# Low parts of five weights moved to POOL and new keys turned into rows on VectorE, in a two-layer streaming encoder step on one Trainium2 core

## The reference

```python
def _layer(x, l, P, past_k, past_v, s_gla0, s_ret0):
    h = _rms_norm(x, P['ffn1_norm_pre'][l])
    x = x + 0.5 * _rms_norm(_swiglu(h, P['ffn1_w_up'][l], P['ffn1_w_down'][l]), P['ffn1_norm_post'][l])
    h = _rms_norm(x, P['mix_norm_pre'][l])
    m, k_rows, v_rows, s_gla, s_ret = _mixer(h, l, P, past_k, past_v, s_gla0, s_ret0)
    x = x + _rms_norm(m, P['mix_norm_post'][l])
    h = _rms_norm(x, P['ffn2_norm_pre'][l])
    x = x + 0.5 * _rms_norm(_swiglu(h, P['ffn2_w_up'][l], P['ffn2_w_down'][l]), P['ffn2_norm_post'][l])
    return x, k_rows, v_rows, s_gla, s_ret
```

## Time and profile before

| | us |
|---|---|
| median of 3 runs | 1318.64 |
| lowest, highest | 1318.46, 1318.78 |
| the profiled execution | 1318.82 |
| its span, first to last instruction | 1316.8 |
| TensorE busy in it | 1304.0 |
| VectorE busy | 829.1 |
| ScalarE busy | 632.5 |
| POOL busy | 131.5 |

### The profile page before, as it was taken

How to read it: one execution, slowest core, us unless ns; L and a number is a source line. 1 busy time by engine, 2 the same in 40 slices (tenths; PEclk the granted TensorE clock), 3 DMA queues, 4 the chain that set the end, 5 groups by cost and what they waited for, 6 DMA issues and landing times.

```text
span 1316.8 us, 24524 instructions
## 1 busy us (share of the span) xinstructions
PE 1304.0 (99%) x9456; PEld 1277.6 (97%) x9456; DVE 829.1 (63%) x1303; ACT 632.5 (48%) x1013; POOL 131.5 (10%) x176
## 2 busy tenths in 40 slices
PE   9999999999999999999999999999999999999998
PEld 8999999998999999999999999999989999999998
DVE  7755644687776955553486556337867778565672
ACT  6544443654556644443464444337535575444432
POOL 1000000450011200000030000005400130000000
PEclk9999999999999999999999999999999999999999
DMA  8555565463344555455545555545533355555552
GB/s 230 162 170 166 152 179 145 133 164 81 97 120 128 151 149 154 144 148 148 152 128 145 154 147 154 155 141 148 133 95 95 92 140 174 153 147 147 143 147 82
DMA packets 352026, 187.39 MB, mean 142 GB/s; under 512 B 9016, under 2 KB 348788, under 8 KB 351960
## 3 DMA queue, kind: packets, MB, share of 16 engines
q1 hardware_dynamic: 348376, 177.78, 47.9%
q0 software_dynamic: 2800, 7.85, 1.8%
q10 hardware_dynamic: 784, 0.86, 0.2%
HBM read 180.82 MB, written 4.33 MB: 141 GB/s over the span
## 4 chain that ended last, share of the span: by engine, by line
PE 93%; DVE 4%; POOL 1%; DVEq 1%; ACT 1%; issue 0%; POOLq 0%
PE ps L717 27%; PE ps L718 27%; PE ps L719 27%; PE ps L741 1%; PE ps L744 1%; PE ps L737 1%; POOL x L581 1%; PE ps L1027 1%; DVE w_l L573 1%; PE ps L1072 1%; PE ps L1096 1%; PE ps L952 1%; PE ps L1003 0%; PE ps L922 0%; PE ps L791 0%
## 5 line engine op out<-in xcount | busy, mean ns | idle before, releaser
L717 PE MATMUL ps<-xn_l,w_h 128*128 128x320 f32 x1696 | 531.9, 314 | 0.0
L719 PE MATMUL ps<-xn_h,w_h 128*128 128x320 f32 x1696 | 523.1, 308 | 0.0
L718 PE MATMUL ps<-xn_h,w_l 128*128 128x320 f32 x1696 | 523.0, 308 | 0.0
L573 DVE TENSOR_TENSOR w_l<-raw,w_h 128x1024 fp32r<-128x1024 f32 (+1 forms) x336 | 400.9, 1197 | 139.0 <-ACT w_h L561 138.6
L561 ACT ACTIVATE w_h<-raw 128x1024 fp32r<-128x1024 f32 (+1 forms) x336 | 346.1, 1034 | 208.8 <-DMA raw<-in_ffn_w_down_dram 127.7
L717 PEld LDWEIGHTS ps<-xn_l,w_h 128*128 128x128 f32 x1696 | 318.7, 188 | 3.7 <-issue 1.0
L718 PEld LDWEIGHTS ps<-xn_h,w_l 128*128 128x128 f32 x1696 | 318.7, 188 | 0.8
L719 PEld LDWEIGHTS ps<-xn_h,w_h 128*128 128x128 f32 x1696 | 318.5, 188 | 0.0
L719 PE MATMUL ps<-hid_h,w_h 128*128 128x320 f32 x704 | 217.0, 308 | 0.0
L717 PE MATMUL ps<-hid_l,w_h 128*128 128x320 f32 x704 | 217.0, 308 | 0.0
L718 PE MATMUL ps<-hid_h,w_l 128*128 128x320 f32 x704 | 217.0, 308 | 0.0
(11 more groups left out here) (310 smaller groups left out, 1265.5 us busy)
## 6 DMA issues: line engine op xcount, KB each, us to landing
raw<-in_ffn_w_up_dram SPq DMA_DIRECT2D x172, 512.0 KB, 3.8
raw<-in_ffn_w_down_dram SPq DMA_DIRECT2D x64, 448.0 KB, 3.7
raw<-in_w_in_dram SPq DMA_DIRECT2D x52, 512.0 KB, 3.8
...
```

The costliest lines, as they stand in the source:

```text
L573: dve.tensor_tensor(w_l[s][:, 0:cols], raw[s][:, 0:cols], w_h[s][:, 0:cols], ALU.subtract).then_inc(w_lo, 1)
L717: pe.matmul(out, w_h[s][:, w], xl, start=first, stop=False)
L718: pe.matmul(out, w_l[s][:, w], xh, start=False, stop=False)
L719: return pe.matmul(out, w_h[s][:, w], xh, start=False, stop=last)
```

## The change

- VectorE makes the token rows of the new keys. The new entry `rows` n transposes, in blocks of 32x32, 32 features of two heads' keys for all tokens: four instructions for the prompt (one for each 32 tokens of a block) and two for the sample. Eight entries, `rows` 0 to 7, take the place of `tok` 0 to 3. POOL's stores wait for `rows` 7 as well as for `tok` 7.
- POOL makes the low parts of tiles 18, 20, 22, 24 and 26, each in its queue at the end of tile n - 5. VectorE waits for POOL's counter before it makes the next tile's low part, and counts `w_lo` up for both, so that it stays in order. VectorE's low part of output tile 1 (number 28) moves behind `att_a` 9.
- `ret_dec` stands ahead of k-blocks 0 to 5 of tile 13 and of level 8. Tile 14 is cut at 4 and 6, not at 2 and 5.
- In `opening` and in `out`, TensorE waits for the low parts tile by tile and not for all four; in the mixer's opening `stat_x` stands two k-blocks later.
- In a spread the third matmul, which is for the sample's block, has 64 columns and not 128.
- At the start of the kernel the first gains are transposed and copied ahead of the first block of x, and two small loads are issued behind the first piece of the sample's x.

The diff, cut to its core:

```diff
+POOL_LOW = (18, 20, 22, 24, 26)
 ...
-       ("part", 12, 3, 8), ("level", 7), ("ketok",), ("part", 13, 0, 5), ("level", 8), ("ret_dec",), ("part", 13, 5, 8),
+       ("part", 12, 3, 8), ("level", 7), ("ketok",), ("ret_dec",), ("part", 13, 0, 5), ("level", 8), ("part", 13, 5, 8),
...
-    + [("att_t", 8), ("att_s", 10), ("att_a", 9), ("tok", 7)] + P8[25][:1] + [("att_o", 8), ("squares", "b")] + P8[25][1:]
+    + [("att_t", 8), ("att_s", 10), ("att_a", 9), ("tok", 7)] + P8[25][:1] + [("att_o", 8), ("squares", "b"), ("rows", 6)] + P8[25][1:]
...
                 for kind, *arg in SCHEDULE:
                     n = arg[0] if arg else None
-                    if kind == "weight":
+                    if kind == "part" and arg[2] == KD and n + 5 in POOL_LOW:
+                        u = U_MIX + n + 5
+                        s = slot(l, u)
+                        pool.wait_ge(w_hi, l * UNITS + u + 1)
+                        pool.tensor_tensor(w_l[s][:, :], raw[s][:, :], w_h[s][:, :], ALU.subtract).then_inc(pool_low, 1)
+                    elif kind == "weight":
...
-                    elif kind == "tok" and n == 7:
+                    elif kind == "rows" and n == 7:
                         after(pool, l, "act", "tok7")
+                        after(pool, l, "dve", "rows7")
                         then_pass(pool)
...
-                pe.wait_ge(w_lo, l * UNITS + u0 + OPENING)
                 for t in range(OPENING):
+                    pe.wait_ge(w_lo, l * UNITS + u0 + t + 1)
...
-                    if t == OPENING - 1:
-                        stat_x(l, m)
                     for i in range(KD // 2, KD):
+                        if t == OPENING - 1 and i == (KD - 2 if u0 == U_MIX else KD // 2):
+                            stat_x(l, m)
...
-                    mm = pe.matmul(ps_rs[:, TOK[i]:TOK[i] + P], inv[:, i:i + 1].broadcast_to([P, P]), C("ident"),
+                    at = 64 if i == 2 else 0
+                    mm = pe.matmul(ps_rs[:, TOK[i] + at:TOK[i] + P], inv[:, i:i + 1].broadcast_to([P, P]), C("ident")[:, at:P],
                                    start=True, stop=True)
...
+                elif kind == "rows":
+                    j, q = n // 4, n % 4 * 32
+                    tiles = slice(PLACE[DKK[2 * j]], PLACE[DKK[2 * j + 1]] + 1, 2)
+                    for p in range(0, P, 32):
+                        new = dk_tok[p:p + 32, 0:2, 2 * j:2 * j + 2, q:q + 32].rearrange("p i h d -> p h i d")
+                        old = z[q:q + 32, tiles, 0:T_P].rearrange("p h (i t) -> p h i t", i=2)[:, :, :, p:p + 32]
+                        i = dve.transpose(new, old)
+                    for p in (64, 96):
+                        i = dve.transpose(dk_tok[p:p + 32, 2, 2 * j:2 * j + 2, q:q + 32], z[q:q + 32, tiles, TOK[2] + p:TOK[2] + p + 32])
+                    mark("dve", i, f"rows{n}")
...
                             z_tile(v)
-                            lo(dve, l, U_MIX + v + 4)
+                            if v + 4 not in POOL_LOW and v != 24:
+                                if v + 3 in POOL_LOW:
+                                    dve.wait_ge(pool_low, l * len(POOL_LOW) + POOL_LOW.index(v + 3) + 1)
+                                    dve.sem_inc(w_lo, 1)
+                                lo(dve, l, U_MIX + v + 4)
                     else:
                         mixer_step(l, kind, arg[0] if arg else None)
+                        if (kind, *arg) == ("att_a", 9):
+                            lo(dve, l, U_OUT + 1)
```

More of the change, by code:

```diff
@@ L89 @@
        ("weight", 7), ("level", 5), ("part", 11, 6, 8), ("part", 12, 0, 3), ("gla_keys",), ("tok", 11), ("level", 6),
-       ("part", 12, 3, 8), ("level", 7), ("ketok",), ("part", 13, 0, 5), ("level", 8), ("ret_dec",), ("part", 13, 5, 8),
-       ("ret_kt", 0), ("part", 14, 0, 2), ("gla_o", 0), ("gla_o", 1), ("ret_kt", 1), ("part", 14, 2, 5), ("ret_s", 0),
-       ("part", 14, 5, 8)]
-    + [("tok", 0), ("att_s", 0)] + P8[15][:1] + [("tok", 4)] + P8[15][1:]
+       ("part", 12, 3, 8), ("level", 7), ("ketok",), ("ret_dec",), ("part", 13, 0, 5), ("level", 8), ("part", 13, 5, 8),
@@ L94 @@
+       ("ret_kt", 0), ("part", 14, 0, 4), ("gla_o", 0), ("gla_o", 1), ("ret_kt", 1), ("part", 14, 4, 6), ("ret_s", 0),
+       ("part", 14, 6, 8)]
+    + [("att_s", 0)] + P8[15][:1] + [("tok", 4)] + P8[15][1:]
     + [("att_s", 1), ("att_a", 0), ("ret_s", 1)] + P8[16]
-    + [("att_t", 0), ("att_s", 2), ("att_a", 1)] + P8[17][:1] + [("att_o", 0), ("ret_o", 0)] + P8[17][1:]
-    + [("ret_o", 1), ("att_t", 1), ("att_s", 3), ("att_a", 2)] + P8[18][:1] + [("att_o", 1), ("ret_mu", 0)] + P8[18][1:]
-    + [("ret_mu", 1), ("att_t", 2), ("att_s", 4), ("att_a", 3)] + P8[19][:1] + [("att_o", 2), ("tok", 1)] + P8[19][1:]
@@ L98 @@
-    + [("att_t", 3), ("tok", 5), ("att_s", 5), ("att_a", 4)] + P8[20][:1] + [("att_o", 3)] + P8[20][1:]
-    + [("att_t", 4), ("att_s", 6), ("att_a", 5)] + P8[21][:1] + [("att_o", 4), ("tok", 2)] + P8[21][1:]
-    + [("att_t", 5), ("squares", "g"), ("att_s", 7), ("att_a", 6)] + P8[22][:1] + [("att_o", 5), ("tok", 6)] + P8[22][1:]
-    + [("att_t", 6), ("att_s", 8), ("att_a", 7)] + P8[23][:1] + [("att_o", 6), ("tok", 3), ("squares", "a")] + P8[23][1:]
+    + [("att_t", 0), ("att_s", 2), ("att_a", 1)] + P8[17][:1] + [("att_o", 0), ("ret_o", 0), ("rows", 0)] + P8[17][1:]
@@ new lines @@
+    + [("ret_o", 1), ("att_t", 1), ("att_s", 3), ("att_a", 2)] + P8[18][:1] + [("att_o", 1), ("ret_mu", 0), ("rows", 1)] + P8[18][1:]
+    + [("ret_mu", 1), ("att_t", 2), ("att_s", 4), ("att_a", 3)] + P8[19][:1] + [("att_o", 2), ("rows", 2)] + P8[19][1:]
+    + [("att_t", 3), ("tok", 5), ("att_s", 5), ("att_a", 4)] + P8[20][:1] + [("att_o", 3), ("rows", 3)] + P8[20][1:]
+    + [("att_t", 4), ("att_s", 6), ("att_a", 5)] + P8[21][:1] + [("att_o", 4)] + P8[21][1:]
+    + [("att_t", 5), ("squares", "g"), ("att_s", 7), ("att_a", 6)] + P8[22][:1] + [("att_o", 5), ("tok", 6), ("rows", 4)] + P8[22][1:]
@@ L102 @@
+    + [("att_t", 6), ("att_s", 8), ("att_a", 7)] + P8[23][:1] + [("att_o", 6), ("squares", "a"), ("rows", 5)] + P8[23][1:]
     + [("att_t", 7), ("att_s", 9), ("att_a", 8), ("stat", "a"), ("root", "a")] + P8[24][:1] + [("att_o", 7)] + P8[24][1:]
-    + [("att_t", 8), ("att_s", 10), ("att_a", 9), ("tok", 7)] + P8[25][:1] + [("att_o", 8), ("squares", "b")] + P8[25][1:]
+    + [("att_t", 8), ("att_s", 10), ("att_a", 9), ("tok", 7)] + P8[25][:1] + [("att_o", 8), ("squares", "b"), ("rows", 6)] + P8[25][1:]
@@ L106 @@
     + [("att_t", 10), ("hi", 2), ("hi", 3), ("stat", "b"), ("root", "b"), ("lo", 2), ("lo", 3), ("att_o", 10), ("att_t", 11), ("gates", 0), ("gates", 1),
-       ("out", 0), ("spread", 0), ("spread", 1), ("att_o", 11), ("lo", 0), ("lo", 1), ("squares", "c"), ("out", 1), ("spread", 4),
+       ("out", 0), ("spread", 0), ("spread", 1), ("att_o", 11), ("lo", 0), ("lo", 1), ("rows", 7), ("squares", "c"), ("out", 1), ("spread", 4),
        ("spread", 6), ("out", 2), ("lo", 4), ("stat", "c"), ("root", "c"), ("lo", 6), ("out", 3), ("spread", 5), ("spread", 7),
@@ L151, in milestones @@
             dve.append("ret_dec")
+        elif kind == "rows":
+            dve.append(f"rows{n}")
         elif kind == "att_s":
@@ L1125, in mixer_step @@
                         for i in range(3):
-                            mm = pe.matmul(ps[:, bank, TOK[i]:TOK[i] + P], inv_h[:, n - 4, i:i + 1].broadcast_to([P, P]), C("ident"),
-                                           start=True, stop=True)
+                            at = 64 if i == 2 else 0
+                            mm = pe.matmul(ps[:, bank, TOK[i] + at:TOK[i] + P], inv_h[:, n - 4, i:i + 1].broadcast_to([P, P]),
+                                           C("ident")[:, at:P], start=True, stop=True)
                     mark("pe", mm, f"spread{n}")
```

12 lines of the change are left out of this document (8 added, 4 removed).

## The result

The changed kernel takes 1326.1 us (median; 1324.6 to 1329.8) against 1318.7 for the kernel before: a ratio of 1.0061, 95% interval 1.0051 to 1.0071 (the two medians alone give 1.0056). It is slower by 7.4 us, where 1.4 were forecast and the range ended at 1322.6. The profiled execution is the longest of them, 1329.79 with a span of 1328.0, 11.2 more than before. One execution of all that follow, one of the small parts alone, took 1401.7 us at a granted clock of 0.851; no ratio and no reading uses it.

A forecast was written before the change was run, and what follows sets the result against it. TensorE, busy 1304.0 of 1316.8 us, was taken as the bound. A layer: +1.14 + 0.99 - 0.5 - 0.4 - 2.2, about -1.0; twice that and 0.5 back made 1.4 us slower, 1320.0 us, range 1315.0 to 1322.6.

The forecast's parts named there:

- the small parts: Both layers together: opening's waits tile by tile, sum of x, a spread's shorter third matmul, wait before `tok` 0: 0.5 gained.
- `ret_dec`, 1.14: Ahead of level 8: VectorE's `ret_dec` falls into its idle time, so TensorE's hole at `ret_kt` goes, gaining 1.14 us a layer.
- `tok` 0 to 3, 0.33 each: Attention stage: four transposing steps a layer removed from TensorE, 0.33 us each, 1.32 in all; 0.99 counted, for `tok` 0 to 2.
- The sum of x: Mixer's opening: TensorE's hole of 0.5 + 0.16 us a layer closes, but the wait comes back at `logit`: gain 0 here.
- The cost of a `rows` step, 1.7: VectorE: four transposes of 32x128 and two of 32x64 with a fixed part take 1.7 us, kept between 1.1 and 1.8.
- the rival of cheap transposes: VectorE: a `rows` step takes 0.7 us, so `rows` 6 fits and `spread` 5 loses 1.2: 1316.7 us; 15%.
- POOL's low part: POOL: one 1024-column low part takes 2.15 us, by proportion from 512 columns; upper end 3.5.
- the rival with a slow POOL: POOL: a low part takes 3.5 us, `att_t` 4 waits 1.9 and other tiles lose 0.4 a layer: 1323.6 us; 17%.
- Tile 20, 0.5: Attention: POOL's low part holds back VectorE's, so TensorE waits at `att_t` 4, losing 0.5 us a layer (0 to 1.0).
- Tile 23 to `out`, 0.4: Up to the output projection's first step: the moved low part and `rows` 6 delay VectorE's `att_a` 10, losing 0.4 us a layer.
- `spread` 5, 2.2: In front of `root` c: `rows` 7 and POOL's four stores delay TensorE's `spread` 5, losing 2.2 us a layer, 0.6 the stores' place.

The follow-up runs named there:

- filled run: Changed kernel with extra TensorE matmuls filling two holes, 10 ahead of `att_t` 10 and 16 ahead of `spread` 5: 1324.35 us.

## Why the prediction was wrong, step by step

The table has TensorE's times between marks of the first layer, read from its timelines. The filled run stands for the changed kernel at full clock. The last column is what the prediction had.

| from, to | before | changed | filled | gain, filled | forecast |
|---|---|---|---|---|---|
| first tile of the first up projection, `att_t` 3 | 313.44 | 311.27 | 311.28 | +2.16 | +1.80 |
| `att_t` 3, `att_t` 4 | 4.84 | 6.52 | 6.32 | -1.48 | -0.5 |
| `att_t` 4, `att_t` 9 | 28.59 | 27.50 | 27.57 | +1.02 | +0.33 |
| `att_t` 9, `att_t` 10 | 5.14 | 6.93 | 6.84 | -1.70 | -0.4, with the next step of `out` |
| `att_t` 10, `spread` 5 | 11.86 | 15.46 | 14.60 | -2.74 | -2.2 |
| sum | | | | -2.74 | -0.97 |

In the second layer the filled run's sum is -2.26, since `att_t` 4 waits 0.91 there and not 1.47. The three losses rest on these rows of the changed kernel, VectorE's and POOL's, to be read beside the earlier trace rows:

```profile
350.66 0.48 DVE L1818 SCALAR_TENSOR_TENSOR probs<-probs,tiny 128x256 f32<-128x256 f32 x1
...
378.56 1.22 DVE L577 TENSOR_TENSOR w_l<-raw,w_h 128x1024 fp32r<-128x1024 f32 x1
...
379.95 1.25 DVE L1840 STREAM_TRANSPOSE dk_tok<-z 32x128 f32<-32x128 f32 x4
...
381.73 0.49 DVE L1924 TENSOR_TENSOR z<-ps,rs 128x320 f32<-128x320 f32 x1
...
385.09 0.48 DVE L1818 SCALAR_TENSOR_TENSOR probs<-probs,tiny 128x256 f32<-128x256 f32 x1
...
396.39 0.49 DVE L1842 STREAM_TRANSPOSE dk_tok<-z 32x64 f32<-32x64 f32 x2
...
397.50 0.80 POOL L689 DMA_DIRECT2D out_new_k_prompt_dram<-dk_tok  x1 [7.63 <-issue]
...
398.81 0.15 DVE L1876 TENSOR_SCALAR var_h<-ps 128x3 f32<-128x3 f32 x1
...
400.14 0.89 POOL L696 TENSOR_TENSOR inv_h<-var_h,minus_half 128x3 f32<-128x3 f32 x1
```

- **`ret_dec`, 1.14: right.** The hole of `ret_kt` went, nothing took its place here, and the run that puts it back shows that it is worth that up to tile 20; at the end of the layer 0.5 and 1.2 of it are left.
- **`tok` 0 to 3, 0.33 each: right**, 0.27 to 0.33 for `tok` 1 to 3 in the traces, and 0.48 for `tok` 0 with the 0.13 for which TensorE had stood ahead of it.
- **The sum of x: right.** TensorE was 1.4 us further at the end of the mixer's opening and lost it at `logit`. With the other small parts it nets nothing.
- **The cost of a `rows` step, 1.7: right** (1.77 to 1.80), and with it the rival of cheap transposes is out. The rate that the prediction turned down for its 1.7 ns a column was right, though: the lengths 256, 128 and 64 lie on 1.04 ns a column, and the fixed 170 ns of each of the six instructions make the step dear. POOL's low part was 10% low at 2.15; at 2.4 it is far from the 3.5 of the rival with a slow POOL, though `att_t` 4 waited nearly the 1.9 that this rival gave it.
- **Tile 20, 0.5: the first step that failed; 1.5 in the filled run, 1.7 in the changed one.** The mechanism was named, and VectorE was even a little earlier than forecast: its L1818 ended at 351.14, not at 351.6. What failed is "TensorE wants that for `att_t` 4 at 351.36, less the 0.33 of `tok` 1: 351.0". TensorE wanted it at 349.5, 1.8 before the old time, because the 1.8 that the sum counts as gained ahead of tile 20 had come in. "VectorE reaches its own low part at about 347.1, as before" failed too: it came to its L577 at 346.43 (345.10 where `rows` 2 stands elsewhere), and POOL began at 345.45, not at 346.1. So POOL was a microsecond ahead and held L577 for 1.3; with `rows` 2 out of the way the two met within 0.1, and the hold was 2.2.
- **Tile 23 to `out`, 0.4: the step that failed worst.** The forecast had `att_a` 10 end at 385.4; it ended at 385.57. On the clock of before every mark of this stretch was right within 0.25: the low part's end, tile 25's copy-out, `att_a` 10, and L754 at 389.24 in the filled run. But "L744 starts at 389.0 instead of 388.62" is a loss of 0.4 against the old clock, at a place where TensorE was by then 1.25 ahead (`att_t` 9 at 378.70, not 379.95). The sum took the 0.4 and also kept the lead. Worked out between marks, VectorE's way from `att_a` 9 to `att_a` 10 grew by the low part (1.15) and `rows` 6 (1.75) less the 0.92 that it sat idle, 2.0; `att_t` 10 waited 1.66, and 1.7 was the term. Some of it had come back ahead of it: `att_t` 9 waits 0.22 (0.32 in the filled run) where it waited 0.74, and this and the 0.33 of `tok` 3 are the third line's 0.7 over the forecast.
- **`spread` 5, 2.2: right in kind, 2.6 measured**, 0.8 the stores and 1.8 `rows` 7. POOL's first store began 0.6 after `rows` 7 had ended (397.50 against 396.88), which the forecast had at 0; why it waited so long is not shown. The stores' place was put at 0.6 of the loss.
- **The clock: missing.** 1.8 us of the median, and most of the spread between executions.

Both failed steps are one: a loss was measured against the old clock, while the sum kept the lead that TensorE had by then. At full clock TensorE's matmuls in the filled run lie 0.6 us behind those of the kernel before at the kernel's first tiles, 3.45 behind the first mixer and 5.8 behind the second. So the two layers lose 2.85 and 2.35, 5.2 together, where 1.4 were forecast with the small parts. Of these 3.8, 1.8 are the first layer's sum, 1.3 the second's, 0.5 the small parts, which gave 0.3 at most, and 0.2 lie outside the marks. The 0.6 at the start is not a cost of the change: that offset was between -0.5 and 0.65 in the profiled executions of all kernels. Together that is the 4.35 by which the filled run is above the forecast; the clock adds 1.8 and makes it the 6.1 to 6.2 of the changed kernel. One might say that the gain ahead of tile 20 is lost whatever one does, but the run with `ret_dec` back refutes this. Why the hole at `att_t` 4 in the second layer is 0.81 in some executions and 1.26 or 1.4 in others is not settled; it goes with how close POOL's start and L577's fall.
